# In the expert stage, VectorE weighs and copies a block's down products ahead of the block's last weight split, not behind it

## The reference, cut to what matters

```
ids, gates = route(t, w_router, router_bias)          # two experts of one group for each token
...                                                   # tokens sorted by expert, padded to blocks of 128
def expert_block(args):
    xb, e = args
    return (jax.nn.silu(xb @ w_gate[e]) * (xb @ w_up[e])) @ w_down[e]
yb = lax.map(expert_block, (buf.reshape(n_blocks, MOE_BLOCK, D), block_e))
y = yb.reshape(-1, D)[dest] * gates.reshape(-1)[order][:, None].astype(t.dtype)
return jnp.zeros_like(t).at[tok].add(y)
x = x + m_lat[5] * ffn.reshape(x.shape)
```

## Time and profile before

| | |
|---|---|
| median of three runs | 2204.32 us (2199.68 to 2204.64) |
| the profiled execution | 2199.41 us, its span from first to last instruction 2197.7 us |
| granted TensorE clock, mean of the span | 0.961 |
| busy: PE, DVE, ACT, POOL | 2036.9, 1663.0, 1185.4, 536.7 us |
| expert stage, first down product to last | 1240.9 to 2130.1 us |
| last copy of the experts ends | 2134.1 us |
| `combine` begins | 2151.2 us |

### The profile page before, as it was taken

How to read it: one execution, slowest core, us unless ns; L and a number is a source line. 1 busy time by engine, 2 the same in 40 slices (tenths; PEclk the granted TensorE clock), 3 DMA queues, 4 the chain that set the end, 5 groups by cost and what they waited for, 6 DMA issues and landing times. The chain is left out here.

```text
span 2197.7 us, 38487 instructions
## 1 busy us (share of the span) xinstructions
PE 2036.9 (93%) x12690; PEld 1692.2 (77%) x12690; DVE 1663.0 (76%) x2132; ACT 1185.4 (54%) x1564; POOL 536.7 (24%) x537
## 2 busy tenths in 40 slices
PE   4999999989999989999995899999999999999970
PEld 3998888877777768888873688888888888888860
DVE  3555545555777687777766799999999999999973
ACT  3433333344555523333333677777777777777753
POOL 1000000000010033333221243433334333333332
PEclk8999999999999979999996899999999999999995
DMA  9443334355988799999937374788888599799957
GB/s 303 160 143 128 128 128 155 134 188 189 338 308 298 258 301 340 296 330 293 326 98 267 97 244 99 257 275 298 287 282 291 172 312 374 252 354 319 369 147 315
DMA packets 219973, 541.34 MB, mean 246 GB/s; under 512 B 15968, under 2 KB 56923, under 8 KB 213339
## 3 DMA queue, kind: packets, MB, share of 16 engines
q1 hardware_dynamic: 186856, 428.68, 54.7%
q0 software_dynamic: 30512, 102.77, 17.5%
q10 hardware_dynamic: 2499, 8.45, 1.0%
HBM read 404.26 MB, written 135.59 MB: 246 GB/s over the span
## 5 line engine op out<-in xcount | busy, mean ns | idle before, releaser
L736 PE MATMUL pf<-x_hi,wide 128*128 128x256 f32 x1152 | 243.8, 288 | 10.7 <-DVE x_lo L863 10.7
L2592 DVE TENSOR_TENSOR w_lo_e<-w_ups,w_hi_e 128x2048 fp32r<-128x2048 f32 x102 | 233.4, 2288 | 26.0 <-ACT w_hi_e L2475 25.3
L2475 ACT ACTIVATE w_hi_e<-w_downs 128x2048 fp32r x100 | 191.9, 1920 | 84.9 <-PE pu_e L2542 79.7
L2592 DVE TENSOR_TENSOR w_lo_e<-w_gates,w_hi_e 128x2048 fp32r<-128x2048 f32 x103 | 235.1, 2284 | 3.2 <-ACT w_hi_e L2475 1.7
L2592 DVE TENSOR_TENSOR w_lo_e<-w_downs,w_hi_e 128x2048 fp32r<-128x2048 f32 x100 | 224.7, 2288 | 7.9 <-issue 5.5
L2475 ACT ACTIVATE w_hi_e<-w_gates 128x2048 fp32r x101 | 193.8, 1920 | 54.4 <-PE pd_e L2542 53.4
L2475 ACT ACTIVATE w_hi_e<-w_ups 128x2048 fp32r (+1 forms) x102 | 196.1, 1923 | 33.3 <-issue 26.8
L736 PE MATMUL pf<-x_lo,wide 128*128 128x256 f32 x720 | 204.3, 284 | 0.0
L736 PEld LDWEIGHTS pf<-x_hi,wide 128*128 128x128 f32 x1152 | 191.6, 193 | 15.8 <-issue 15.5
L2449 POOL DMA_INDIRECT x_mid<-choice,to_e x50 | 140.6, 2812 | 138.0 <-DVE choice L2639 135.9
L2428 POOL COPY idx_e<-toks 128x1 int32 (+1 forms) x54 | 64.0, 1185 | 429.2 <-DMA x_mid<-choice,to_e 259.7
(11 more groups left out here) (466 smaller groups left out, 4820.5 us busy)
## 6 DMA issues: line engine op xcount, KB each, us to landing
w_gates<-in_w_gate_dram SPq DMA_DIRECT2D x32, 2048.0 KB, 11.8
w_ups<-in_w_up_dram SPq DMA_DIRECT2D x32, 2048.0 KB
w_downs<-in_w_down_dram SPq DMA_DIRECT2D x32, 2048.0 KB, 9.7
recs<-tok_rec SPq DMA_DIRECT2D x17, 968.0 KB, 7.9
qk<-in_w_mod_dram SPq DMA_DIRECT2D x16, 1024.0 KB, 6.3
raws<-a_rows SPq DMA_DIRECT2D x16, 1024.0 KB, 7.0
qk_rec<-qk SPq DMA_DIRECT2D x14, 1024.0 KB, 3.9
qk<-qk_rec SPq DMA_DIRECT2D x14, 1024.0 KB, 8.2
```

The lines of the kernel that those rows point to most:

```text
L736: mm = pe.matmul(pf[n % 2][:, f % 2, :], a[f][:, k, :], b[:, k, :], start=(k == 0 and j == 0), stop=(k == KT - 1 and j == 2))
L2475: act.activation(w_hi[:, n:n + 1, :], raw(part, half, place), ACT.Copy).then_inc(hi_done, 1)
L2592: dve.tensor_tensor(w_lo[:, n:n + 1, :], raw(part, half, place), w_hi[:, n:n + 1, :].bitcast(F32), ALU.subtract).then_inc(lo_done, 1)
```

## The change

The two operations of the copy, with their three waits, now stand between piece 9 and piece 10, not behind piece 10. Nothing is added or taken away, and the other engines' programs are the same.

```diff
@@ -2631,13 +2631,13 @@
                 piece(8)
                 features(b + 2, u)
                 piece(9)
-                piece(10)
                 dve.wait_ge(used, b * 6 + 8)
                 dve.wait_ge(y_free, b + 1)
                 dve.wait_ge(to_ready, b + 1)
                 for n in range(2):
                     dve.scalar_tensor_tensor(out=yb[:, 512 * n:512 * n + 512], in0=pd[n][:, :], scalar=to[u][:, 1:2].bitcast(F32),
                                              in1=gate_bc[:, 512 * n:512 * n + 512], op0=ALU.mult, op1=ALU.mult).then_inc(y_copied, 1)
+                piece(10)
             pairs(dve, body)
```

## The result

The changed kernel took 2208.55 us (median of 20 runs, 2202.78 to 2210.87), the kernel before 2202.55 us (20 runs, 2197.43 to 2204.64). The ratio is 1.0027, with a 95% interval of 1.002 to 1.0033: 6.0 us slower, small, but clear of noise. A second round on the same chip as the experiments gave 1.0038 (1.0024 to 1.0051).

A forecast was written before the change was run, and what follows sets the result against it. TensorE was taken to bound the expert stage, so 0 us within the blocks and 0.93 us less behind the last: 2204.32 - 0.93 = 2203.4 us, called no change; range 2197.5 to 2206.5 us.

The forecast's parts named there:

- The copy starts 5.87 us behind down, `h` 11.59: Within a block: the copy moves 1.64 us earlier, to 5.87 us behind the start of down; `h` starts 0.15 us later.
- The table load behind the copy costs nothing: Within a block: piece 10's table load, now behind the copy, is hidden by the copy's 1.32 us; priced at nothing.
- From the start of `h` to the end of `h_lo` 5.68 to 5.93 us, so 0.5 us is left.: Within a block: `h_lo` ends by 1618.80 to 1619.05, down begins at 1619.56; so 0 us for the 49 steps.
- The earlier trace as the proof: In a block before the change, `h` came 11.92 us behind down, yet the next down began on time, after 18.03 us.
- 0.93 us won at the end, with a trigger of 2.85 us beside piece 10: Behind the last block: the copy starts 2.20 us earlier, piece 10 holds up the trigger, 0.93 us is won; chance 0.77.
- the first rival: Behind the last block: piece 10 doesn't hold the trigger, so the whole 2.20 us is won, 2202.1 us; chance 0.10.
- The second rival: Within blocks: late landings delay `y_free`, the copy and VectorE's chain; TensorE waits 1.0 us in 20 steps, 2224 us; chance 0.07.

The follow-up runs named there:

- The early load: The changed kernel with VectorE's table load for pieces 6 and 7 moved from behind the wait for up to ahead of piece 5; 2201.77 us, ratio 1.0002.
- the late trigger: The changed kernel with GpSimd's trigger of the scatter held until piece 10 is done; 2200.27 us, ratio 0.9991.
- a probe: The changed kernel with three unused table loads added on ScalarE behind piece 7's high part; one execution, 2206.81 us.

## Why the prediction was wrong

It said 2203.4 us in a range of 2197.5 to 2206.5, and no change; measured were 2208.55 us and 6.0 us more than before. Point by point:

- *The copy starts 5.87 us behind down, `h` 11.59*: 5.86 to 5.90 and 11.58 to 11.62 in all blocks. Right.
- *The table load behind the copy costs nothing*: piece 10 follows 1.32 us behind the copy in every block. Right, and I looked at the wrong load.
- *From the start of `h` to the end of `h_lo` 5.68 to 5.93 us, so 0.5 us is left.* This is the step that failed, on two counts. The gap of 0.60 to 0.83 us behind `h` was taken over from blocks of the kernel before as if it were a property of the instruction. It holds a register load, and the load's length depends on what the DMA engines do. The change moved the scatter by 1.65 us and laid it over this load; in the worst step the 5.93 us became 6.81. The early load, the late trigger, and the kernels without a scatter or with a gather each show it. The second count is smaller: the next down does not start when `h_lo` ends, but 0.22 us later (1496.27 to 1496.49 above). I had left that out, though I had counted such a reaction at the copy. With it some 0.3 us was left, not 0.5. Steps with a quick load hold even so: with no scatter all 48 fit.
- *The earlier trace rows as the proof*: a late `h` had been no harm there. True, but there the load began at 1342.8, 0.2 us ahead of `h`, while the piece before it still ran, took 0.30 us, and no scatter was under way. It proved the slack for the old time of the scatter only.
- *0.93 us won at the end, with a trigger of 2.85 us beside piece 10*: the trigger took 2.86, and from PE's last matmul to `combine` it is 19.92 us, not 21.02: 1.10 won. Right, if 0.2 us small, and the first rival, 2.20, is out. The Trainium skill (DMA: Bandwidth & Descriptors, SWDGE vs HWDGE vs iDMA) names only 2-port modes as what locks GpSimd out; here a trigger beside a two-tensor subtraction takes 2.86 us against 1.60 in an idle stretch, as the rows of before had it. That the subtraction is the cause was argued from this pair, and no run tried it.
- *The second rival, slower through the scatter's landing and `y_free`*, named the right transfer and the wrong way. The copy never waited for a landing, and GpSimd's own waits for landings fell from 259.7 to 84.2 us. The earlier scatter did harm at the other end, at its start.

The loss by the sum: the loads are 16.6 us longer in total, and 6.86 us came through to TensorE. The difference, 9.7 us, is put down to cover and spare time of the chain; it was not measured by itself.

## What to carry to other kernels

Between a wait and the next instruction look for what the sequencer must fetch first: a register load that stands behind the wait has hardly any cover, and its length is no constant. Hoist such loads over the wait; here one line did it, and with it the change costs nothing. And when a transfer is moved, ask not only when it lands and what it frees, but what short, bare operations of other engines now fall beside it; here ScalarE's load had shown the price all along, in a place where it cost nothing.

## What the runs showed of the hardware

A register load from SBUF (four bytes of the table `plan`) took 0.26 to 0.34 us on ScalarE, VectorE and SyncE in nearly all places, also while all 16 DMA engines were busy with weights coming into SBUF, or with gathers. Around a scatter that adds, it took up to 1.2 us, on VectorE and on ScalarE alike, and up to 1.76 on a probe behind another load; beside the packets of a scatter that doesn't add, VectorE's took 0.55 to 0.59 us.

The Trainium skill (DMA: Bandwidth & Descriptors, Latency and other measured facts) gives such a load a floor of about 600 ns; here most take half of that. The Trainium skill (SBUF — State Buffer, SBUF: two separate sides) says that engine ports and DMA ports can't contend. For the pieces of VectorE that holds in these traces: their medians are 2.28 to 2.29 us with the scatter and without. The register load is slowed by a DMA all the same; by which port it reads, no run here shows.

Read packet by packet, 16 of the 27 slow loads of the changed kernel ran while the engines were on the scatter's packets. The other 11 began while weights were still moving, and the scatter's first packet came 0.9 to 2.1 us after the load had begun; four loads with the packet 1.0 to 1.3 us away stayed under 0.45 us, and with a gather on its way in the scatter's place none was slow. What holds up the load ahead of the scatter's packets was not tried and stays open.
